# GLA's two directions in one pass per head pair

## What is computed

```python
def _gla_chunkwise(q, k, v, la, S0):
    def step(st, inp):
        qc, kc, vc, lc = inp
        g = jnp.cumsum(lc, axis=2)
        dec = jnp.exp(jnp.where(causal, g[:, :, :, None, :] - g[:, :, None, :, :], -jnp.inf))
        att = jnp.einsum('bhtd,bhsd,bhtsd->bhts', qc, kc, dec)
        o = jnp.einsum('bhtd,bhde->bhte', qc * jnp.exp(g), st) + jnp.einsum('bhts,bhse->bhte', att, vc)
        ...
of, Sf = _gla_chunkwise(gq, gk, gv, la[:, 0], S0[:, 0])
ob, Sb = _gla_chunkwise(flip(gq), flip(gk), flip(gv), flip(la[:, 1]), S0[:, 1])
og = (of + flip(ob)).transpose(0, 2, 1, 3)
```

## Time and profile before

| | us |
|---|---|
| median of three runs | 2017.23 (2015.67 to 2018.09) |
| the profiled execution | 2019.61 |
| its span | 2017.6 |
| PE busy | 1947.4 (97%) |
| DVE busy | 700.5 (35%) |
| ACT busy | 467.3 (23%) |
| POOL busy | 119.9 (6%) |
| granted clock of PE, mean | 0.989 of full |
| weights and other DMA | 421.69 MB, mean 209 GB/s |

### The profile page before, as it was taken

One profiled execution on the slowest core, in us unless ns is written; L12 is line 12 of the kernel. 1 busy time (PEld: TensorE's weight loads), 2 busy tenths in 40 slices (PEclk: granted clock), 3 DMA queues, 4 the chain that ended last, 5 costly groups with the idle time before them and its releaser, 6 DMA issues. The chain is left out here.

```text
span 2017.6 us, 29193 instructions
## 1 busy us (share of the span) xinstructions
PE 1947.4 (97%) x12530; PEld 1054.9 (52%) x12530; DVE 700.5 (35%) x1675; ACT 467.3 (23%) x910; POOL 119.9 (6%) x159
## 2 busy tenths in 40 slices
PE   6999999999999989999989999999999998999997
PEld 3445566566555554444445565665665555444443
DVE  1394655233211131222234956633331113122213
ACT  2312334343100121001133133434420012111112
POOL 0001101000000020000020030010000002000002
PEclk9999999999999989999999999999999998999998
DMA  9661531413466549999963223132113244999994
GB/s 401 224 249 58 190 144 58 146 68 141 169 236 242 224 167 366 388 390 390 402 227 116 84 90 130 47 113 103 70 63 125 101 177 181 347 393 390 395 403 153
DMA packets 48625, 421.69 MB, mean 209 GB/s; under 512 B 6272, under 2 KB 6416, under 8 KB 25456
## 3 DMA queue, kind: packets, MB, share of 16 engines
q1 hardware_dynamic: 33696, 369.44, 47.6%
q0 software_dynamic: 8080, 26.78, 3.9%
q10 hardware_dynamic: 6720, 23.60, 3.3%
HBM read 389.08 MB, written 28.61 MB: 207 GB/s over the span
## 5 line engine op out<-in xcount | busy, mean ns | idle before, releaser
L774 PE MATMUL psum<-hT,ring 128*128 128x384 f32 x1088 | 366.5, 490 | 2.0 <-ACT pc L1327 1.9
L1022 PE MATMUL psum<-hT,ring 128*128 128x384 f32 x1024 | 343.4, 489 | 0.0
L774 PEld LDWEIGHTS psum<-hT,ring 128*128 128x128 f32 x1088 | 202.2, 190 | 144.3 <-issue 17.3
L1022 PEld LDWEIGHTS psum<-hT,ring 128*128 128x128 f32 x1024 | 191.9, 190 | 130.2
L1037 PE MATMUL psum<-pc,ring 128*128 128x384 f32 x512 | 177.5, 490 | 0.0
L2213 DVE TENSOR_TENSOR ytok<-pc,psum 128x384 f32<-128x384 f32 x32 | 17.7, 554 | 336.6 <-ACT pc L1583 336.6
L1993 DVE TENSOR_TENSOR mva<-mva,psum 128x384 f32<-128x384 f32 x48 | 26.6, 554 | 308.4 <-PE psum L1037 259.5
L2205 DVE COPY scr<-psum 64x512 f32<-64x512 f32 (+1 forms) x180 | 91.8, 510 | 114.8 <-PE psum L1168 113.2
L1037 PEld LDWEIGHTS psum<-pc,ring 128*128 128x128 f32 x512 | 94.0, 190 | 71.8 <-issue 15.1
L1780 DVE SCALAR_TENSOR_TENSOR pc<-pc,par 128x384 f32<-128x384 f32 x240 | 127.2, 616 | 0.0
L777 PE MATMUL psum<-ring,hT 128*128 128x512 f32 x288 | 125.6, 593 | 0.0
(11 more groups left out here) (359 smaller groups left out, 2043.3 us busy)
## 6 DMA issues: line engine op xcount, KB each, us to landing
ring<-we_in SPq DMA_DIRECT2D x48, 2048.0 KB, 18.7
pc<-we_in SPq DMA_DIRECT2D x48, 2048.0 KB, 18.7
ring<-wch_in SPq DMA_DIRECT2D x18, 2048.0 KB, 8.8
ring<-wgate_in SPq DMA_DIRECT2D x16, 2048.0 KB, 8.4
ring<-wmod_in SPq DMA_DIRECT2D x18, 1024.0 KB, 6.1
pc<-wmod_in SPq DMA_DIRECT2D x24, 768.0 KB, 6.2
ring<-wbr_in SPq DMA_DIRECT2D x16, 1024.0 KB, 8.3
ring<-wtok_in SPq DMA_DIRECT2D x6, 2048.0 KB, 8.8
```

What stands on the lines that cost most here:

```text
L774: mm = pe.matmul(F[:, 0:T], wv[:, k, n * P:(n + 1) * P], hT[:, k, :], start=k == 0, stop=k == KD - 1)
L1022: mm = pe.matmul(bank(5 + n % 2)[:, 0:T], wv[:, k, (n % 4) * P:(n % 4 + 1) * P], hT[:, k, :], start=k == 0, stop=k == KD - 1)
```

## The change

One pass per head pair, both directions at once. There is one table of keys and one of queries per pair: the key halves of the forward direction and those of the backward direction are each other's complement at every level, so both fit in one table, and the same holds for queries. `differences(u)` still runs per direction, 14 subtractions, and writes into both tables; `factors` and `scale` run per table, `scale` with one multiplication of the whole table (two for the second) by k or q repeated over the levels. `scores(pair)` multiplies keys by queries: the diagonal part stays 48 products per tile and now gives both directions, `beside` makes both off-diagonal squares, so twice the products per call (24 and 12). One mask for both directions, with the factor 2 on the equal-token level, since both directions hold the diagonal. One score tile, filled wholly by the copies, so the fill with zero is gone; `beside_copies` copies twice the squares. One value product (`attend`) per pair. Cross product, state and the share of the initial state stay per direction. The order is written anew on PE, ACT and DVE: all three tok units come before the transposes, the first part stands alone, and units n = U_LOOP + 4 pair to n + 3 are the four units of a pair, of which n and n + 1 are split. On ACT factors(1, 0) stands ahead of the copy of n + 2, and ACT's sigmoid of the mLSTM gate moves ahead of the first exponentials. POOL's fetch of rotary partners waits for the last `ga_done` under its new number.

```diff
--- before.py
+++ after.py
@@
-        g_att = [pc_flat[:, DKK * 4 * T + d * 6 * P:DKK * 4 * T + (d + 1) * 6 * P].rearrange("p (x t) -> p x t", x=6)
-                 for d in range(2)]
+        g_att = pc_flat[:, DKK * 4 * T + 6 * P:DKK * 4 * T + 12 * P].rearrange("p (x t) -> p x t", x=6)
...
@@ tensor engine
-                def scores(u):
+                def scores(pair):
+
+                    k_of, q_of = g_zl
...
-                                        ks, qs = z[lv][r, c], z[lv][r, c]
+                                        ks, qs = k_of[lv][r, c], q_of[lv][r, c]
...
+                        lv = 5 if w == 32 else 6
                         for t in range(NT):
-                            for j in range(P // (2 * w)):
-                                s0 = 2 * w * j + (w if d else 0)
-                                t0 = 2 * w * j + (0 if d else w)
+                            for j in range(P // w):
+                                s0, t0 = w * j, w * (j ^ 1)
...
-                unit(U_GLA)
-                unit(U_GLA + 1)
-                pe.wait_ge(m_out.sem, m_out.at(l, 8))
-                pe.wait_ge(st_copied.sem, st_copied.at(l, 8))
-                finish_transposes(l, 0)
-                unit(U_GLA + 2)
-                pe.wait_ge(fin_done.sem, fin_done.at(l, 1))
-                passes[0][0]()
-                unit(U_GLA + 3, passes[0][1])
...
+                def cross(u):
...
+                def state(u):
...
+                def from_before(u):
+                    pair, d = divmod(u, 2)
+                    tq, tk = (2, 1) if d == 0 else (1, 2)
                     if u == 2:
                         pe.wait_ge(go_copied.sem, go_copied.at(l, 2))
...
+                def attend(pair):
+                    pe.wait_ge(gatt_ready.sem, gatt_ready.at(l, pair + 1))
+                    for hh in range(2):
+                        head = pair * 2 + hh
+                        for t in range(NT):
+                            mm = pe.matmul(bank(4 + hh)[:, tok(t)], g_att[:, hh * 3 + t, :], gv[:, t, head * P:(head + 1) * P],
+                                           start=False, stop=True, skip_group_check=True)
+                        mm.then_inc(go_done.sem, 1)
+
+                unit(U_GLA)
+                unit(U_GLA + 1)
+                unit(U_GLA + 2)
+                pe.wait_ge(m_out.sem, m_out.at(l, 8))
+                pe.wait_ge(st_copied.sem, st_copied.at(l, 8))
+                finish_transposes(l, 0)
+                unit(U_GLA + 3)
+                pe.wait_ge(fin_done.sem, fin_done.at(l, 1))
...
+                for pair in range(2):
+                    u, n = 2 * pair, U_LOOP + 4 * pair
+                    first, second, third = scores(pair)
+                    first()
+                    unit(n, second)
+                    cross(u)
+                    unit(n + 1, third)
+                    state(u)
+                    from_before(u)
+                    cross(u + 1)
+                    unit(n + 2)
+                    state(u + 1)
+                    from_before(u + 1)
+                    unit(n + 3)
+                    attend(pair)
...
@@ scalar engine
+                def factors(pair, table):
+
+                    ac.wait_ge(gd_ready.sem, gd_ready.at(l, 2 * pair + 2))
+                    for _, z in g_z[table]:
                         o = ac.activation(z, z, ACT.Exp, scale=1 / 16)
                     o.then_inc(gx_ready.sem, 1)
...
+                unit_copy(U_GLA)
+                ac.wait_ge(unit_copied.sem, unit_copied.at(l, units_to("ch", MO)))
+                ac.activation(pc[:, MO, :, :], pc[:, MO, :, :], ACT.Sigmoid).then_inc(mo_open.sem, 1)
+                ac.preload_act_table_set(LN_EXP)
+                factors(0, 0)
+                unit_copy(U_GLA + 1)
+                finish(0)
+                factors(0, 1)
+                cross_factors(0)
+                unit_copy(U_GLA + 2)
+                unit_copy(U_GLA + 3)
+
+                for pair in range(2):
+                    u, n = 2 * pair, U_LOOP + 4 * pair
+                    unit_copy(n)
+                    cross_copies(u)
+                    cross_factors(u + 1)
+                    beside_copies(pair, 32)
+                    unit_copy(n + 1)
+                    state_copies(u)
+                    beside_copies(pair, 64)
+                    cross_copies(u + 1)
+                    if pair == 0:
+                        factors(1, 0)
+                    unit_copy(n + 2)
+                    state_copies(u + 1)
+                    if pair == 0:
+                        factors(1, 1)
+                    diagonal_copies(pair)
+                    unit_copy(n + 3)
+                    if pair == 0:
+                        cross_factors(2)
...
@@ vector engine
-                        ve.tensor_tensor(z[:, :, high], middle, sums[:, :, high], ALU.subtract)
-                        o = ve.tensor_tensor(z[:, :, low], sums[:, :, low], middle, ALU.subtract)
+                        ve.tensor_tensor(k_of[:, :, high], middle, sums[:, :, high], ALU.subtract)
+                        o = ve.tensor_tensor(q_of[:, :, low], sums[:, :, low], middle, ALU.subtract)
...
+                def scale(pair, table):
+
+                    ve.wait_ge(gx_ready.sem, gx_ready.at(l, 2 * pair + table + 1))
+                    for levels, z in g_z[table]:
+                        src = pc[:, GQK, pair if table else 2 + pair, :].rearrange("p (a t) -> p a t", a=1)
+                        o = ve.tensor_tensor(z, src.to_broadcast([P, len(levels), T]), z, ALU.mult)
+                    if table:
+                        o.then_inc(gz_ready.sem, 1)
...
                 differences(0)
+                differences(1)
                 finish_sums(l, 0, vals[:, 0:1536])
                 cross_differences(0)
                 finish_norm(l, 0)
...
-                for d in range(2):
-                    step(ve.memset(g_att[d], 0.0))
...
+                cross_scale(0)
+                for pair in range(2):
+                    u = 2 * pair
+                    if pair:
+                        ve.wait_ge(gsum_ready.sem, gsum_ready.at(l, pair))
+                    masked(pair, 0)
+                    cross_freed(u)
+                    cross_differences(u + 1)
+                    cross_scale(u + 1)
+                    masked(pair, 1)
+                    if pair == 0:
+                        for of in (2, 3):
+                            differences(of)
+                    ve.wait_ge(gm_ready.sem, gm_ready.at(l, pair * 4 + 4))
+                    if pair:
+                        ve.wait_ge(gatt_ready.sem, gatt_ready.at(l, pair))
                     ve.tensor_reduce(g_c, g_m.rearrange("p (x l t) -> p x t l", x=6, l=NLEV), AX.X, ALU.add)\
                       .then_inc(gsum_ready.sem, 1)
+                    if pair == 0:
+                        cross_freed(1)
+                        cross_differences(2)
+                        for table in range(2):
+                            scale(1, table)
+                        cross_scale(2)
...
@@ masks
+    m = np.zeros((P, NLEV, SUB))
+    for lv in range(NLEV - 1):
+        w = 1 << lv
+        m[:, lv] = (i // (2 * w) == j // (2 * w)) & (i // w != j // w)
+    m[:, NLEV - 1] = 2.0 * (i == j)
+    put("lev", m)
```

More of the change, by code:

```diff
@@ L258, in hybrid_step @@
         cond = cc("cond").rearrange("p (k c) -> p k c", k=KD)
-        lev = [cc("lev_f"), cc("lev_b")]
+        lev = cc("lev")
         tri_f = cc("tri_f")
@@ L938, in _ @@
                     pe.transpose(bank(7)[:, 256:384], g_kd, ident).then_inc(gs_t.sem, 1)
-                    unit(U_LOOP + 2 * u, passes[u][2])
+                def state(u):
+                    pair = u // 2
                     pe.wait_ge(gs_tc.sem, gs_tc.at(l, u + 1))
@@ L944, in _ @@
                               start=True, stop=True).then_inc(gs_done.sem, 1)
-                    if u < 3:
-                        unit(U_LOOP + 2 * u + 1, passes[u + 1][0])
-                        passes[u + 1][1]()
-                    else:
-                        unit(U_DIFF)
+                def from_before(u):
+                    pair, d = divmod(u, 2)
+                    tq, tk = (2, 1) if d == 0 else (1, 2)
                     if u == 2:
                         pe.wait_ge(go_copied.sem, go_copied.at(l, 2))
-                    pe.wait_ge(gatt_ready.sem, gatt_ready.at(l, u + 1))
-                    for hh in range(2):
-                        head = pair * 2 + hh
-                        for t in range(NT):
-                            pe.matmul(bank(4 + hh)[:, tok(t)], g_att[d][:, hh * 3 + t, :], gv[:, t, head * P:(head + 1) * P],
-                                      start=(d == 0 and t == 0), stop=False, skip_group_check=True)
                     for t in (1, 2):
@@ L1473, in _, with beside_copies @@
-                    ac.wait_ge(gsum_ready.sem, gsum_ready.at(l, u + 1))
+                def beside_copies(pair, w):
```

(30 more changed lines are left out.)

150 lines of the change are left out of this document (40 added, 110 removed).

## The result

The changed kernel takes 1985.68 us in the median of four runs (1982.34 to 1986.32), the kernel before 2017.66; the ratio is 0.9832 with a 95% interval of 0.9806 to 0.9858. The forecast was 1987.9. The profiled execution took 1986.17 us, its span 1984.4, so the profiled executions differ by 33.4 us and the medians by 32.0, where the sum said 29.3.

The account below looks back on a forecast made before the run. PE's own instructions were taken as the time; terms summed to 14.6 us per layer, 29.3 in all, which off the median 2017.23 gave 1987.9 us, range 1984 to 1991 at chance 0.70, with rivals up to 1998.

Parts of the forecast that it names:

- first parts: PE's 48 score products of one token tile: from 4 to 2 per layer at 1.35 us, 2.70 us removed.
- second parts: PE's 48 score products plus 32-wide beside products: 4 x 1.54 become 2 x (1.35 + 0.62), 2.22 us removed per layer.
- third parts: PE's 48 score products plus 64-wide beside products: 4 x 1.85 become 2 x (1.35 + b), 3.20 us removed per layer.
- value products: PE's value products, six in a set: from 4 sets to 2 per layer at 1.54 us, 3.08 us removed.
- waits: PE's waits for the bank copy (0.96), first cross product (0.67) and transposes (0.64) go: 2.27 us per layer.
- units and their splits: PE units with a part inside: from 8 split to 4 per layer at 0.29 us each, 1.16 us removed.
- state steps: PE's state steps in the passes: same in number, they only move, so no saving counted.
- b: Cost of the doubled 64-wide beside products in a third part: 0.75 us taken, bounds 0.50 and 1.00.
- Covers: DVE and ACT finish ahead of PE by 0.6 us (front, layer 0), 1.5, 1.8 and 2.0; nothing becomes late.
- The slower rival: DVE's two wide multiplications in an unmeasured shape take about three times 5.9 us, giving 2028 us; chance 0.03.
- The sequencer: Rival: longer second parts run PE's sequencer dry, four gaps giving 8.0 us instead of 2.5, 1993.4 us; chance 0.10.
- Given back in the experts: Rival: weight arrival set by DMA engines alone returns all 29.3 us as PE waits in the experts, 2017; chance 0.05.

Follow-up runs that it names:

- e7: Changed kernel with the six 64-wide products on one column half issued before the six on the other; 1984.76 us in a single execution.
- e10: Changed kernel with the second part behind unit n instead of inside it; 1978.44 us, ratio 0.9827 to the kernel before.
- e12: Changed kernel with the second part behind unit n and the third behind unit n + 1, neither inside; 1979.53 us, ratio 0.9829 to the kernel before.
- e3: Kernel before with only PE's new front order: three tok units ahead of the transposes, first and second part of pass 0 without a unit between; 2022.48 us.
- e8: Changed kernel with three extra DVE reductions, 3.8 us of unused work, ahead of the differences of pair 1; 1989.20 us in a single execution.
- e11: Changed kernel with one extra DVE reduction of 1.1 us ahead of the differences of pair 1; 1984.00 us in a single execution.
- e4: Changed kernel with every narrow diagonal product issued twice onto the same place; 2018.94 us, ratio 1.0012 to the kernel before.
- e5: Changed kernel with all three parts of a pair in one run ahead of unit n, no unit split; 2001.02 us, ratio 0.9919 to the kernel before.
- e9: Changed kernel unaltered, timed again on another chip; 1983.96 us, ratio 0.9850 to the kernel before.
- e2: Kernel before without the value product of the backward direction; 2010.36 us, ratio 0.9971 to the kernel before.
- e1: Kernel before without the narrow diagonal products of the backward direction; 1996.07 us, ratio 0.9898 to the kernel before.

## Why the prediction was right, point by point

The sign, the mechanism and the place were right, and the time lies 2.2 us below the forecast. The sum itself was 4.1 us short of the two profiles and 2.7 short of the medians. The stretch per layer, without the sequencer's gaps, became 16.5 us shorter in both layers (17.7 less 1.2 us of gaps in layer 0; 15.7 and 0.8 us more gaps in layer 1), to 14.6 in the sum. Its terms:

| term, us per layer | sum | measured |
|---|---|---|
| first parts | 2.70 | 2.70 |
| second parts | 2.22 | 4 x 1.54 - 2 x 1.77 = 2.62 |
| third parts | 3.20 | 4 x 1.85 - 2 x 1.87 = 3.66 |
| value products | 3.08 | 6.04 - 2.77 = 3.27 |
| waits | 2.27 | 2.27 |
| units and their splits | 1.16 | 48.9 - 47.7 = 1.2 |
| state steps | nothing | 4 x (0.60 - 0.52) = 0.3 |
| tok units and transposes | nothing | 22.2 - 21.9 = 0.3 |
| not assigned | | 0.2, what is left of 16.5 |

- **Second and third parts.** The step that failed is the price of the doubled beside products: 0.62 and 0.75 us taken, 0.42 and 0.52 measured, 0.9 us per layer. For the second part the reading of the rows was wrong: 0.31 is the share of 24 records in 120 of 1.54 us, but the sum sets it on top of a first part of 1.35, and 1.54 less 1.35 is 0.19. Doubled, that is 0.38, near the 0.42. For the third part the lower bound of b, 0.50, was the right one; e7 shows that the added products cost little.
- **Splits.** The term has the right size, in part by luck. 0.29 us was read off one unit with a first part inside and taken for all eight. A unit with a third part inside took 5.36 us, 0.12 over the whole one of 5.24; the earlier trace rows had it (286.49 to 289.17 and 291.02 to 293.70). One with a second part inside took 5.56 to 5.63. That gives less than 1.16 for the splits alone; whole units that ran in 5.16 and not 5.24 made up for it. e10 puts 0.2 on a second part's split and e12 nothing on a third part's.
- **What the sum left out.** It priced state steps, tok units and transposes as unchanged. They gave another 0.6 us per layer, because a state step took 0.52 in place of 0.60 and the three tok units now run in one piece.
- **Waits.** All three kinds went as said, and e3 shows two of them go by the front order alone.
- **Covers.** 1.5 us was worked out for the copy of unit n + 2, 1.4 measured (e8, e11, e12). This was the sum's best tested step. At the front 0.6 was worked out for layer 0; in the trace the step of DVE that signals `fin_done` ends at 257.5 and PE comes there at 258.27, so 0.7. The covers of 1.8 and 2.0 us were not tested beyond that no wait came. The slower rival fell with the wide multiplication at 3.00 us.
- **The sequencer.** This was a rival with 0.10, and the runs show it to be real, though the changed kernel met it only with 1.0 and 1.3 us. The prediction left the gaps "as they are", which happened to hold (2.7 us with one of 0.2 that the earlier trace rows leave out, to 2.4); that was luck and not understood. The reason given against it, that most second parts show no gap, did not rule it out: the closer the narrow parts follow each other, the more gaps come, as e3, e4, e5 and e10 show with 7.1, 17.5, 15.4 and 0 us. But how close they stand is not all that decides. In every profile of the changed kernel's order (e7, e8, e9 and e11 too) each layer has one gap, in the second part of pair 0 and at the same matmul each time, and the same products in the same order in pair 1 have none. The gaps stand at fixed places 256 instructions apart (e4), and the DMA engines are busier in pair 0. Which of the two, the place or the load, spares pair 1 was not tested, nor whether e10 is free of gaps by its spacing alone or also by where those places fall in it.
- **Given back in the experts.** Nothing was: the stretches have all of the difference, and PE's waits for expert weights are 4.2 us before and 4.1 after.

## What to carry to other kernels

Where PE is busy nearly all the time, price a change by start-to-start rows of the very shapes, and check the other engines' chains against PE's time between the same two handovers; here this gave the cover within 0.1 us. Take the added cost of a few products as the difference between two rows, not as their share of one. Count instructions too: a run of small products can be limited by how fast instructions arrive, so put long matmuls between such runs rather than joining them. A reordering that looks free by the price list can cost more than it was meant to gain: e3 lost 5.9 us for 3.4 expected, e5 lost 15 for 3.0 expected.

## What the runs showed of the hardware

- 64x32 products of 32 columns on alternating parts of the array issue at 12.8 ns a record while instructions are there (128 in 1.64 us, e5). When they run out, 256 instructions (128 such records and their weight loads) arrive every 3.5 to 3.7 us, less than half that rate.
- In these passes PE's sequencer stops only at places a multiple of 256 instructions apart, semaphore instructions counted (e4: 512, 1024, 512; e5: 256, 768, 256; the kernel before, layer 0: 1536).
- Such a gap is longer under DMA load: 4.2 and 3.8 us with the DMA engines at 1.00 and 0.82, 1.6 and 1.5 us with them idle, for equal runs (e4). The load alone was not varied.
- After the gap of 4.2 us in e5 the granted clock was 0.50, the 1.2 GHz level, and it was 0.75 over the 9.9 us behind the one in e4. After a gap of 2.0 us it fell in one profile (e2, 0.79 over 8 us) and not in two others (before, e1), after one of 1.6 us in e7 and not in e8 and e11. So a gap has a second price that varies from run to run.
- A second set of six 64x64 products on the other column half costs 0.02 us in turn with the first set, and 0.18 as a block behind it (e7).
